# A two-block layer on one core: where the first drive waits for the state-space parameters, and in which chunks the gating's layer norm stands

## The reference

```python
def s5_scan(u, a_re, a_im, log_dt, b_re, b_im, c_re, c_im, d_skip):
    ...
    lam_bar = jnp.exp(lam * dt)
    b_bar = ((lam_bar - 1.0) / lam)[..., None] * b
    bu = jnp.einsum('gpc,blgc->blgp', b_bar, ug.astype(jnp.complex64))
    ...
    _, h = lax.associative_scan(combine, (a, bu), axis=1)
    y = jnp.einsum('gcp,blgp->blgc', c, h).real + d_skip.astype(f32) * ug

def chunked_spatial_gating(u, v, ln_g, ln_b, w_s, b_s):
    v = layer_norm(v, ln_g, ln_b)
    vc = v.reshape(bsz, n, CHUNK_2, HEADS_A, DH_A)
    ...
    mixed = jnp.einsum('hts,bnshd->bnthd', w, vc) + b_s.T[None, None, :, :, None]
    return u * mixed.reshape(bsz, s, WIDTH_A)
```

## Time and profile before

| | |
|---|---|
| median of 3 runs | 2691.19 us (2690.69 to 2691.64) |
| the profiled execution | 2691.55 us |
| its span, first to last instruction | 2690.3 us |
| mean granted TensorE clock | 0.989 |
| PE, matmul | 2634.7 us busy |
| DVE | 1640.2 us busy |
| ACT | 844.9 us busy |
| POOL | 414.4 us busy |

### The profile page before, as it was taken

The page is one execution under the profiler, slowest core; times in us unless marked ns, Lnnn a source line. Parts: engine busy times, 40 slices in busy tenths (PEclk is TensorE's granted clock), DMA queues, the critical chain, the costliest instruction groups (busy, mean ns, idle before and its releaser), DMA issues.

```text
span 2690.3 us, 29964 instructions
## 1 busy us (share of the span) xinstructions
PE 2634.7 (98%) x11904; PEld 2158.3 (80%) x11904; DVE 1640.2 (61%) x2170; ACT 844.9 (31%) x1140; POOL 414.4 (15%) x311
## 2 busy tenths in 40 slices
PE   7989999999999999999999999989999999998997
PEld 5868888888888888888888888877888888887786
DVE  6677888887888766445444775556555553233434
ACT  5222222222222222222322332232556554232321
POOL 4024334343343421000000000020000000000001
PEclk9999999999999999999999999989999999999998
DMA  4333333333333333667555675523222222322333
GB/s 167 102 100 115 107 108 100 117 117 102 115 104 121 131 122 118 211 204 241 188 197 191 208 241 182 188 99 130 95 79 79 79 79 87 115 93 74 111 124 110
DMA packets 119707, 353.07 MB, mean 131 GB/s; under 512 B 15376, under 2 KB 22800, under 8 KB 119568
## 3 DMA queue, kind: packets, MB, share of 16 engines
q1 hardware_dynamic: 119568, 351.16, 39.2%
HBM read 321.68 MB, written 23.07 MB: 128 GB/s over the span
## 4 chain that ended last, share of the span: by engine, by line
PE 96%; DVE 2%; issue 1%; ACT 0%; DMA 0%; POOL 0%; SPq 0%; DVEq 0%; POOLq 0%; ACTq 0%
PE bank L500 29%; PE bank L502 28%; PE bank L501 28%; PE bank L654 2%; PE bank L656 2%; PE bank L655 2%; DVE hL L1373 1%; PE bank L697 1%; PE bank L687 1%; PE bank L548 1%; PE bank L558 1%; PE bank L680 0%; PE bank L678 0%; PE bank L493 0%; DVE X L1762 0%
## 5 line engine op out<-in xcount | busy, mean ns | idle before, releaser
L1106 DVE TENSOR_TENSOR WL<-W,WH 128x1024 fp32r<-128x1024 f32 x456 | 596.0, 1309 | 551.5 <-ACT WH L791 550.3
L791 ACT ACTIVATE WH<-W 128x1024 fp32r<-128x1024 f32 x456 | 480.2, 1056 | 1025.0 <-PE bank L502 785.3
L500 PE MATMUL bank<-hH,WH 128*128 128x512 f32 x1792 | 702.1, 392 | 14.2 <-DVE hL L1373 14.1
L501 PE MATMUL bank<-hL,WH 128*128 128x512 f32 x1792 | 699.8, 391 | 0.0
L502 PE MATMUL bank<-hH,WL 128*128 128x512 f32 x1792 | 699.8, 390 | 0.0
L500 PEld LDWEIGHTS bank<-hH,WH 128*128 128x128 f32 x1792 | 337.4, 188 | 97.0 <-DVE hL L1373 11.5
L502 PEld LDWEIGHTS bank<-hH,WL 128*128 128x128 f32 x1792 | 337.3, 188 | 70.9
L501 PEld LDWEIGHTS bank<-hL,WH 128*128 128x128 f32 x1792 | 337.7, 188 | 70.2
L500 PE MATMUL bank<-h2H,WH 128*128 128x512 f32 x640 | 253.4, 396 | 0.1
L502 PE MATMUL bank<-h2H,WL 128*128 128x512 f32 x640 | 250.1, 391 | 0.0
L501 PE MATMUL bank<-h2L,WH 128*128 128x512 f32 x640 | 249.9, 390 | 0.0
(11 more groups left out here) (258 smaller groups left out, 3623.4 us busy)
## 6 DMA issues: line engine op xcount, KB each, us to landing
W<-in_w SPq DMA_DIRECT2D x336, 512.0 KB, 3.7
W<-in_ada SPq DMA_DIRECT2D x96, 512.0 KB, 4.4
W<-in_wa SPq DMA_DIRECT2D x32, 512.0 KB, 3.8
W<-in_wo SPq DMA_DIRECT2D x32, 512.0 KB, 3.9
W<-in_wvv SPq DMA_DIRECT2D x32, 512.0 KB, 3.7
W<-in_wb SPq DMA_DIRECT2D x16, 512.0 KB, 3.7
URAW<-U SPq DMA_DIRECT2D x96, 64.0 KB, 3.1
XS<-in_xT SPq DMA_DIRECT2D x8, 512.0 KB, 9.0
```

Source lines behind the costliest of these rows:

```text
L500: e.matmul(o, wh, xh, start=first, stop=False)
L501: e.matmul(o, wh, xl, start=False, stop=False)
L791: e.activation(WH[:, n % NB, :], W[:, i % NW, :], ACT.Copy).then_inc(sem["hi"], 1)
L1106: e.tensor_tensor(WL[:, s, :], W[:, plan.item_of[n] % NW, :], WH[:, s, :].bitcast(F32), ALU.subtract).then_inc(sem["lo_v"], 1)
```

## The change

In PE's generator the wait for the parameters moves from ahead of `drive(0)` into `readout(0)`. DVE runs the third and fourth piece of its layer norm behind the low halves of slots 4 and 5, no longer of slots 6 and 8. ACT runs its second piece (squares 2 and 3) behind the high half it makes at slot 3 and its third (the square root) behind that of slot 4, no longer at slots 4 and 6. All the instructions are the same as before.

```diff
@@ -553,6 +553,8 @@
                 e.wait_ge(*nth("ssm_v", 4 * ut + 3))
                 if ut >= 1:
                     e.wait_ge(*nth("skip", ut - 1))
+                else:
+                    e.wait_ge(sem["prm_v"], counts["param"])
                 for z in range(2):
                     for i in range(4):
                         mm = e.matmul(bank[3][32 * i:32 * i + 32, :], CB[:, z, 4 * ut + i, :], HH[i][:, z, :],
@@ -560,7 +562,6 @@
                 mm.then_inc(sem["ssm_out"], 1)
 
             yield
-            e.wait_ge(sem["prm_v"], counts["param"])
             drive(0)
             yield
             for j in range(32):
@@ -1063,10 +1064,10 @@
             split_y(i, k)
         for h in range(4, 8):
             for i in range(2):
-                unit()
-                if h > 4 or i > 0:
-                    next(norm, None)
-                unit()
+                for _ in range(2):
+                    unit()
+                    if (h, i) in ((4, 1), (5, 0)):
+                        next(norm, None)
                 gates(h, i)
         for i in range(2, 8):
             split_y(i, 8 + i)
@@ -1727,7 +1728,7 @@
         split_y(1, 9)
         for i in range(16):
             unit()
-            if i in (0, 1, 6, 8):
+            if i in (0, 1, 4, 5):
                 next(norm)
             if 8 <= i < 15:
                 mix(i - 8)
```

## The result

The changed kernel takes 2677.46 us (median of 4 runs, 2676.58 to 2679.30) against 2691.32 us: 13.9 us less, a ratio of 0.995 with a 95% interval of 0.9932 to 0.9967. The forecast was 2673.7 us, in a range up to 2676.8: the sign was right, 17.5 us of gain were forecast and 13.9 came. The profiled execution took 2677.76 us about a span of 2676.5.

What follows compares the result with a forecast made beforehand. TensorE, busy 98%, was taken as the bound, so only its stalls could give time: 12.8 - 3.7 - 1.5 = 7.6 us plus 9.9 us, 17.5 us off the median 2691.19, gives 2673.7 us; range 2670.8 to 2676.8.

Steps and rivals of the forecast that it cites:

- Second part: Layer norm moved forward: scaling done 9.6 us before mix 0 is due, so the whole 9.9 us stall goes.
- First part, removal: Parameter wait leaves drive 0 at chunk 26: the drive runs at 164.4 and all 12.8 us go.
- First part, new stall: PE waits at chunk 30 for DVE's low half 30: 3.7 us, ends 3.1 and 4.3.
- that row of work: DVE from first rotation through multiplications and convolution to low half 30: 7.95 us, begun at 182.3, ending at 190.3.
- the disturbance of the first table: Low half 29 beside POOL's first table operation delays the tables: up to 1.2 us, 0.6 taken.
- The clock: PE's granted clock falls behind the 3.7 us idle time at chunk 30: price 1.5 us, ends 0 and 1.9.
- the slowness of the drive itself: Deducted from the old stall's 1.9 us clock price: drive 0.99 us in place of 0.52, leaving 1.4 us.
- a second short stall: Allowance of 2 us on the upper side of the range for another stall behind chunk 30.
- (a): Stall at chunk 30 is 3.1 us or less and the clock holds: 2671.6 us; chance 0.25.
- (b): Half the gain fails: DVE bounds the first stretch, 2681.3 us, or scaling still late, 2683.7; chance 0.10 with (c).
- (c): Drive 0 meets another wait, so the change does not do what it says: 2681.3 us; chance 0.10 with (b).
- (d): DVE held at the rotation by POOL's tables at every scan step: slower, 2835 us; chance 0.02.

Runs made afterwards that it cites:

- POOL held back: Changed kernel with POOL's tables of step 1 and what follows waiting until DVE has done the convolution of chunk 27: 2678.10 us, ratio 0.995.
- tables left out: Changed kernel with POOL's table operations of step 1 covering 32 columns instead of 512, so that step is not computed: 2670.76 us, ratio 0.9926.
- first part alone: Kernel before with only the parameter wait moved from the first drive to the readout: 2686.73 us against 2690.55, ratio 0.9985.
- scaling in the eighth chunk: Changed kernel with ScalarE's layer norm as before and DVE's scaling at slot 7 instead of 5, variance at slot 6: 2677.91 us, ratio 0.9951.
- the scan two chunks later: Changed kernel with the scan's phases from 22 on two chunks later on every engine, a little denser: 2668.49 us, repeat 2668.34 us.
- the same with the drive later: The scan two chunks later, with the parameter wait kept ahead of drive 0 and that drive at chunk 29: 2667.37 us, ratio 0.9911.
- held back longer: Changed kernel with POOL's tables of step 1 waiting until after DVE's scans of step 0: 2677.99 us, ratio 0.9949.
- convolution first: Changed kernel with DVE's convolution at chunk 27 ahead of the first rotation instead of behind it: 2672.89 us, ratio 0.9931.
- low half first: Changed kernel with DVE making low half 30 right behind low half 29, ahead of the first rotation: 2675.77 us, ratio 0.994.

## Why the prediction was wrong

**Second part, 9.9 us: right** in its working and its size. The squares, the table load and the gate fitted behind slot 3 with 0.7 us to spare (0.5 had been worked out), the 9.6 us in hand were there, and alone the part gave 9.0 us by the medians.

**First part, removal: right.** All 12.8 us at chunk 26 went, drive 0 ran at once, the moved wait holds nothing.

**First part, new stall: right in place and mechanism, wrong in size.** The failing step is "that row of work runs from 186.73 to 193.46 + 1.22, 7.95 us. Begun at 182.3 it ends at 190.3". The row was taken as if its length belonged to it. It depends on what POOL does meanwhile. Before, POOL was ahead and had finished at 191.7, in the middle of the convolution. In the changed kernel POOL begins the tables of step 1 as DVE begins its row, does seven operations beside it, and the row took 10.7 us; with POOL still it is 7.0 (POOL held back; tables left out). That is 2.7 us of the 3.1 us by which the stall was longer. The other 0.4 is the disturbance of the first table, of which 0.6 us was taken and 1.0 came.

The Trainium skill's rule quoted there (SBUF — State Buffer, "Who interferes with whom": exclusion for a whole instruction) was weighed for low half 29 alone. The trace agrees with it there (POOL's 1.05 us became 2.09, not the full 1.2 us more), and it bears on the whole row: the four multiplications with one input in PSUM kept 0.69 us, while the operations with two inputs in SBUF grew (one from 0.69 to 0.91, the two fused ones from 1.54 to 3.08 together). The same section counts a tensor_scalar among the operations that can take both ports; here it went from 0.49 to 2.38. The prediction had the rule at hand and did not put it to the row.

**The clock: right that it falls, too cheap, and in part by luck.** 1.5 us were taken, with 1.9 as the end; 2.4 came: eleven products at 0.43 us. The failing step is "less the slowness of the drive itself ..., which chunk 30 has not". The drive stood in the slow stretch of the old stall, 4.0 us from 175.35 to 179.33; without it other products stand there. The new slow stretch was 4.8 us (194.77 to 199.61), in the first part alone 3.5. So 1.9, the whole price of the old stall, would have been the nearer term, and the falls behind an idle time for a low half cost 1.6 to 2.9 us in these runs.

That 3.7 us of idleness would bring a fall was read from the 2.60 us of the earlier trace rows. That is a poor witness: the clock had been at 0.50 before that idle time and rose in it.

```profile
1788.00:1790.00 2.00, 2.00 (x10) 1.77 (x9) 0.92 (x1) 0.60 (x1) 0.92 (x1) 0.50 0.00 0
...
1791.00:1792.00 1.00, 0.00 (x0) 0.00 (x0) 0.32 (x1) 1.00 (x2) 1.00 (x1) 1.00 0.00 0
```

Behind 3.1 us the clock fell in two kernels and stayed in a third (which then had a fall behind 2.85 us), so the forecast stall of 3.7 us could have gone either way. The idle time of 6.7 us that came had a fall in all three traces that show it (changed kernel, first part alone, scaling in the eighth chunk).

**The balance.** The row is 2.7 us, the first table 0.4 and the clock 0.9 us dearer than forecast, 4.0 together; the median lies 3.8 us above the forecast.

**The range.** The ends of the two terms, 4.3 and 1.9 us, were both passed (6.8 and 2.4); the 2 us for "a second short stall" did not make up for it. The range ended at 2676.8, 0.7 us short.

**The rivals.** (a), the quick case, did not come in the changed kernel; the nearest to it are the three faster executions without the tables of step 1 (2670.4 to 2670.8 us; 2671.6 had been worked out), whose clock was not seen. (b), DVE as the bound of the first stretch, was dismissed because DVE idled 9.39 us: the idle time was real, but the order of the queue made it useless. So 9.2 of the 12.8 us came back in another place. (c) did not come: drive 0 started at once. (d) did not come: no step after the first waits.

Not separated: how much of the clock's price depends on where an idle time falls. And the last 1.1 us between the scan two chunks later and the same with the drive later (2668.49, 2668.34 and 2667.37 us) are within the intervals and are not settled.

## What to carry to other kernels

When a wait is taken off one engine, follow the next wait through the queue of the engine that had been hidden behind it, and time what stands there with its new neighbours: a row of VectorE work is not the same length when GpSimd runs beside all of it. Idle time on a second engine is no slack if ready work is queued behind the instruction that waits; moving that instruction back by one or two steps of the main loop was worth 9 us here, more than twice what removing the wait alone brought (3.8 us). Moving the disturbing work instead only moved the disturbance, at both places that were tried.

## What the runs showed of the hardware

- Beside POOL's operations a 128x512 operation of DVE on one tensor with a scalar took 2.38 us instead of 0.49, two of the fused kind (multiply by a scalar, add a tensor) 3.08 instead of 1.54, a scan up to 3.30 instead of 1.22; multiplications with an input in PSUM kept 0.69. These are one instruction each beside two or more of POOL's, so they are examples and no price list.
- Idle times of nearly the same length cost differently. Behind 3.08 us the granted clock fell to 0.50 in one kernel (POOL held back) and stayed at 1.00 behind 3.06 us in another (held back longer); behind 1.88 us it fell (convolution first), behind 1.23 us it did not. The windows of the one held back longer, columns as above, around its products from 190.63 on:

```profile
188.00:190.00 2.00, 0.00 (x0) 0.00 (x0) 1.97 (x3) 0.72 (x1) 0.00 (x0) 1.00 0.00 0
190.00:192.00 2.00, 1.37 (x6) 1.15 (x7) 1.94 (x4) 0.00 (x0) 0.00 (x0) 1.00 0.23 59
192.00:194.00 2.00, 2.00 (x11) 1.65 (x10) 2.00 (x3) 0.00 (x0) 0.00 (x0) 1.00 0.52 203
```

In the same execution the clock did fall behind a shorter idle time:

```profile
240.29 0.79 PE L500 MATMUL bank<-hH,WH 128*128 128x512 f32 x1 [2.85 <-DVE WL L1107]
240.89 0.63 PE L501 MATMUL bank<-hL,WH 128*128 128x512 f32 x1
```

- The price of a fall, from the end of the idle time to the first product at full speed, was 1.6 us (POOL held back longer, at 240.3), 1.7 (first part alone, convolution first, tables left out), 1.9 (before, with the drive), 1.9 again (low half first), 2.4 (changed), 2.5 (scaling in the eighth chunk) and 2.9 (POOL held back, fourteen slow products). So an idle time of 3.1 us cost 3.1 us in one execution and 6.0 in another.
